# Differential attention on one core: GpSimd's part in the softmax pipeline, the place of a reciprocal, and where TensorE waits for two banks

## What is computed

```python
def diff_attn_rows(q1, q2, k1, k2, v, qpos, kpos, key_real, slopes, lam):
    dist = jnp.abs(qpos[:, None] - kpos[None, :]) * key_real[None, :]
    bias = -slopes[:, None, None] * dist[None]
    s1 = jnp.einsum('bqhd,bkhd->bhqk', q1, k1) * scale + bias
    s2 = jnp.einsum('bqhd,bkhd->bhqk', q2, k2) * scale + bias
    attn = jax.nn.softmax(s1, axis=-1) - lam * jax.nn.softmax(s2, axis=-1)
    return jnp.einsum('bhqk,bkhe->bqhe', attn, v)
```

## Time and profile before

| what | us |
|---|---|
| median of 3 runs | 1567.14 (1566.63 to 1567.72) |
| the profiled execution | 1568.71 |
| its span, first to last instruction | 1567.0 |
| TensorE busy over the span | 1527.6 (97%) |
| VectorE busy | 846.6 (54%) |
| ScalarE busy | 533.5 (34%) |
| GpSimd busy | 242.5 (15%) |
| mean granted TensorE clock | 0.995 |

### The profile page before, as it was taken

How to read it: one execution, slowest core, us unless ns; L and a number is a source line. 1 busy time by engine, 2 the same in 40 slices (tenths; PEclk the granted TensorE clock), 3 DMA queues, 4 the chain that set the end, 5 groups by cost and what they waited for, 6 DMA issues and landing times.

```text
span 1567.0 us, 21117 instructions
## 1 busy us (share of the span) xinstructions
PE 1527.6 (97%) x7380; PEld 1239.3 (79%) x7380; DVE 846.6 (54%) x1521; ACT 533.5 (34%) x942; POOL 242.5 (15%) x190
## 2 busy tenths in 40 slices
PE   7999999999999999999999999999999999999997
PEld 6867886877788888887699778788777888888876
DVE  5577895466554355345754283444665543553454
ACT  5124445533322222222511264444333221321223
POOL 2323334340000000000002373222400000000000
PEclk9999999999999999999999899999999999999999
DMA  6524420033333333322323201210333333333322
GB/s 149 149 54 122 148 58 1 8 89 107 93 94 98 90 94 94 102 87 83 91 81 93 55 15 55 68 54 28 102 99 91 97 94 94 94 94 94 94 81 94
DMA packets 250859, 132.61 MB, mean 85 GB/s; under 512 B 21289, under 2 KB 247717, under 8 KB 250798
## 3 DMA queue, kind: packets, MB, share of 16 engines
q1 hardware_dynamic: 248574, 123.92, 27.9%
q0 software_dynamic: 2144, 7.77, 1.6%
q10 hardware_dynamic: 80, 0.14, 0.0%
HBM read 129.67 MB, written 6.38 MB: 87 GB/s over the span
## 4 chain that ended last, share of the span: by engine, by line
PE 89%; DVE 5%; issue 2%; ACT 2%; DMA 1%; POOL 0%; SPq 0%; DVEq 0%; ACTq 0%
PE psL L1706 60%; PE psL L1845 11%; PE psS L1706 5%; PE psT L1854 2%; PE psL L1973 1%; PE psS L2117 1%; PE psS L1950 1%; PE psS L1880 1%; DMA xin<-in_x 1%; PE psS L1893 1%; PE psS L2057 1%; PE psL L2075 1%; DVE wl L1032 1%; PE psS L2094 1%; PE psS L2058 0%
## 5 line engine op out<-in xcount | busy, mean ns | idle before, releaser
L1706 PE MATMUL psL<-hn,wh 128*128 128x512 f32 x1680 | 529.0, 396 | 1.1 <-POOL wl L573 0.9
L1706 PEld LDWEIGHTS psL<-hn,wh 128*128 128x128 f32 x1680 | 314.1, 188 | 77.3 <-issue 1.4
L697 ACT ACTIVATE wh<-stage 128x1024 fp32r<-128x1024 f32 (+3 forms) x250 | 243.2, 973 | 325.6 <-PE psL L1706 232.8
L1706 PE MATMUL psL<-hn,wl 128*128 128x512 f32 x840 | 330.5, 393 | 0.0
L1032 DVE TENSOR_TENSOR wl<-stage,wh 128x1024 fp32r<-128x1024 f32 (+1 forms) x168 | 201.1, 1197 | 90.9 <-ACT wh L697 86.2
L1706 PE MATMUL psL<-hid,wh 128*128 128x512 f32 x704 | 222.1, 396 | 4.8 <-DVE wl L1032 4.8
L573 POOL TENSOR_TENSOR wl<-stage,wh 128x1024 fp32r<-128x1024 f32 (+2 forms) x82 | 156.8, 1913 | 326.5 <-ACT wh L697 326.5
L1706 PEld LDWEIGHTS psL<-hn,wl 128*128 128x128 f32 x840 | 158.0, 188 | 35.8
L1845 PE MATMUL psL<-hn,wh 128*128 128x512 f32 x496 | 172.8, 429 | 1.9 <-POOL wl L573 1.8
L1706 PEld LDWEIGHTS psL<-hid,wh 128*128 128x128 f32 x704 | 130.8, 187 | 40.7 <-DVE wl L1032 5.9
L1706 PE MATMUL psL<-hid,wl 128*128 128x512 f32 x352 | 138.8, 394 | 0.0
(11 more groups left out here) (381 smaller groups left out, 1982.4 us busy)
## 6 DMA issues: line engine op xcount, KB each, us to landing
stage<-in_w_in SPq DMA_DIRECT2D x54, 512.0 KB, 3.9
stage<-in_w_ffn_gate SPq DMA_DIRECT2D x22, 512.0 KB, 3.8
stage<-in_w_ffn_up SPq DMA_DIRECT2D x22, 512.0 KB, 3.8
stage<-in_w_ff_gate SPq DMA_DIRECT2D x22, 512.0 KB, 3.8
stage<-in_w_ff_up SPq DMA_DIRECT2D x22, 512.0 KB, 3.8
stage<-in_w_out SPq DMA_DIRECT2D x16, 512.0 KB, 3.9
stage<-in_w_ffn_down SPq DMA_DIRECT2D x16, 512.0 KB, 3.8
stage<-in_w_ff_down SPq DMA_DIRECT2D x16, 512.0 KB, 3.9
```

Of the source, the lines that this page charges most:

```text
L697: act.activation(wh[:, b, 0:n], stage[:, b, 0:n], ACT.Copy).then_inc(hi[b], 1)
L1706: ins = pe.matmul(dst, w[:, b, k * P:(k + 1) * P], x[:, part, k, c0:c1], start=k + n == 0, stop=k == kc - 1 and n == 2)
```

## The change

Five edits in the stage df, and the diff below is complete but for context.

- There is a second bias tile: `biasD0` and `biasD1`, used by even and odd blocks. The work on them is cut into units of one head (`bias_unit`), and the unit of block i, from block 2 on, waits only for the end of block i-2. The first three units lie between the `wl` tiles of `qb2`, three more ahead of the stage's steps, and the rest one to a step.
- The copy of the 16 meta columns moves from ScalarE to GpSimd (`stack_maps_meta`).
- GpSimd's eight `bias_window` instructions are spread: two to a step behind the copies of units 2 and 3, one to a step behind those of units 12 to 15. The `wl` tile of `gates2` comes behind all of them, so behind the last unit's copy.
- VectorE takes the reciprocal of unit j-1 between the two maps of unit j, with a semaphore `recip_ok` in place of the link.
- TensorE's wait for the two banks of `psL` moves from the head of the stage to step 3, ahead of the first instruction that writes them.

```diff
--- before.py
+++ after.py
@@ -293,6 +293,7 @@
         PT2, o = at("PT2", [P, 2, NB * P], o)
         m8d, o = at("m8d", [P, 2, P], o)
         vm8, o = at("vm8", [P, 5, NH, META], o)
+        biasD1, o = at("biasD1", [P, 4, NKEY], o)
         assert o <= hn0
 
 
@@ -350,7 +351,8 @@
         vbM, o = at("vbM", [P, NH * HD], o)
         qbT, o = at("qbT", [P, 4, SEQ], o)
         dist, o = at("dist", [P, DIST], o)
-        biasD, o = at("biasD", [P, 4, NKEY], o)
+        biasD0, o = at("biasD0", [P, 4, NKEY], o)
+        biasD = (biasD0, biasD1)
         o1 = o
         biasW, o = at("biasW", [P, NH, META + WIN2 + META], o1)
         vaT, o2 = at("vaT", [P, 4, NKEY], o1)
@@ -433,6 +435,7 @@
         h_sq, h_sq2, hg_hi, hg_lo = [sem(n) for n in "h_sq h_sq2 hg_hi hg_lo".split()]
         biasD_ok, biasW_ok, dist_ok, df_sum, y_sq, lam_e = [
             sem(n) for n in "biasD_ok biasW_ok dist_ok df_sum y_sq lam_e".split()]
+        recip_ok = sem("recip_ok")
         fin_gain, fin_rms, fin_out = sem("fin_gain"), sem("fin_rms"), sem("fin_out")
         fin_t, fin_ok = [sem("fin_t0"), sem("fin_t1")], [sem("fin_ok0"), sem("fin_ok1")]
 
@@ -643,13 +646,21 @@
             pool.iota(dist[:], pattern=[[-1, DIST]], base=3 * P, channel_multiplier=1,
                       allow_small_or_imprecise_dtypes=True).then_inc(dist_ok, 1)
 
-            def bias_block(i):
-
-                if i:
-                    pool.wait_ge(ph["df"]["neg"], 8 * i)
-                for h in range(4):
-                    pool.tensor_scalar(biasD[:, h, META:NKEY], dist[:, 3 * P - P * i:3 * P - P * i + SEQ],
-                                       -(2.0 ** (-8.0 * (h + 1) / 4)), None, ALU.mult).then_inc(biasD_ok, 1)
+            def bias_unit(j):
+
+                i, h = divmod(j, 4)
+                if i >= 2:
+                    pool.wait_ge(ph["df"]["neg"], 8 * (i - 1))
+                pool.tensor_scalar(biasD[i % 2][:, h, META:NKEY], dist[:, 3 * P - P * i:3 * P - P * i + SEQ],
+                                   -(2.0 ** (-8.0 * (h + 1) / 4)), None, ALU.mult).then_inc(biasD_ok, 1)
+
+            def stack_maps_meta(u):
+
+                i, h = divmod(u, 4)
+                pool.wait_ge(df_sum, u + 1)
+                if h == 0 and i >= 2:
+                    pool.wait_ge(ph["df"]["pt"], META_TURN[4][i - 2] + 1)
+                pool.tensor_copy(m8d[:, i % 2, h * META:(h + 1) * META], W6[:, u % 3, 0, 0:META]).then_inc(ph["df"]["meta"], 1)
 
             def bias_window(h0, h1):
                 for h in range(h0, h1):
@@ -664,19 +675,34 @@
             pool.tensor_copy(vm8[:, 4], vbT[:, 0:META].unsqueeze(1).broadcast_to([P, NH, META])).then_inc(vm8_ok, 1)
             low_pair("qa2", 1)
             pool.wait_ge(dist_ok, 2)
-            pool.memset(biasD[:, :, 0:META], 0.0)
-            low_pair("qb2", 0)
-            low_pair("qb2", 1)
-            bias_block(0)
-            bias_block(1)
+            for tile in biasD:
+                pool.memset(tile[:, :, 0:META], 0.0)
+            low("qb2", 0, 0)
+            bias_unit(0)
+            low("qb2", 0, 1)
+            bias_unit(1)
+            low("qb2", 1, 0)
+            bias_unit(2)
+            low("qb2", 1, 1)
+            for j in range(3, 6):
+                bias_unit(j)
+            pool.wait_ge(zeros, 2)
+            stack_maps_meta(0)
+            bias_unit(6)
+            stack_maps_meta(1)
+            bias_unit(7)
             pool.wait_ge(nat_t, 3)
             pool.wait_ge(dist_ok, 3)
             pool.memset(biasW[:, :, 0:META], 0.0)
             pool.memset(biasW[:, :, META + WIN2:], 0.0)
-            bias_window(0, NH // 2)
-            bias_block(2)
-            bias_window(NH // 2, NH)
-            bias_block(3)
+            for u in range(2, 16):
+                stack_maps_meta(u)
+                if 4 <= u < 12:
+                    bias_unit(u + 4)
+                elif u < 4:
+                    bias_window(2 * u - 4, 2 * u - 2)
+                else:
+                    bias_window(u - 8, u - 7)
             lows("gates2")
             lows("br2")
 
@@ -953,15 +979,6 @@
                 if j < 16:
                     for m in range(2):
                         softmax_unit(p, 2 * j + m, W6[:, j % 3, m, :], 2 * j + m)
-                if 2 <= j < 18:
-                    u = j - 2
-                    i, h = divmod(u, 4)
-                    act.wait_ge(df_sum, u + 1)
-                    if u == 0:
-                        act.wait_ge(zeros, 2)
-                    if h == 0 and i >= 2:
-                        act.wait_ge(p["pt"], META_TURN[4][i - 2] + 1)
-                    act.activation(m8d[:, i % 2, h * META:(h + 1) * META], W6[:, u % 3, 0, 0:META], ACT.Copy).then_inc(p["meta"], 1)
                 for n, u, i in turns_at(j - 2, 4):
                     take_turn(p, n, P if u is None else NB * P, PT2)
             units = list(window2_units())
@@ -1591,22 +1608,30 @@
                     take_scaled(name, i, 1, dst[:, 2 * i + 1, :], R, QSCALE)
 
             p = ph["df"]
+
+            def reciprocal_of(u):
+                v.wait_ge(ph["df"]["p"], 2 * u + 2)
+                v.reciprocal(st[:, 6, 0:1], rsum[:, 2 * u + 1:2 * u + 2]).then_inc(recip_ok, 1)
+
             for j in range(16 + 5):
                 if j < 16:
                     i, h = divmod(j, 4)
                     for m in range(2):
                         u = 2 * j + m
+                        if m and j:
+                            reciprocal_of(j - 1)
                         v.wait_ge(p["s"], u + 1)
                         v.wait_ge(biasD_ok, 4 * i + h + 1)
                         if j >= 3 and m == 0:
                             v.wait_ge(p["pt"], TURN[4][j - 3] + 1)
                             v.wait_ge(p["meta"], j - 2)
                         biased(p, u, as_halves(W6[:, j % 3, m, :], NKEY), two_banks(psS[:, 2 * m:2 * m + 2, :], NKEY),
-                               as_halves(biasD[:, h, :], NKEY), -TAKEN, u)
+                               as_halves(biasD[i % 2][:, h, :], NKEY), -TAKEN, u)
+                if j == 16:
+                    reciprocal_of(15)
                 if 1 <= j < 17:
                     u = j - 1
-                    v.wait_ge(p["p"], 2 * u + 2)
-                    dv.link(v.reciprocal(st[:, 6, 0:1], rsum[:, 2 * u + 1:2 * u + 2]))
+                    v.wait_ge(recip_ok, u + 1)
                     dv.link(v.scalar_tensor_tensor(out=st[:, 6, 1:2], in0=rsum[:, 2 * u:2 * u + 1], scalar=st[:, 6, 0:1], in1=neglam[:],
                                                    op0=ALU.mult, op1=ALU.mult))
                     v.scalar_tensor_tensor(out=W6[:, u % 3, 0, :], in0=W6[:, u % 3, 1, :], scalar=st[:, 6, 1:2], in1=W6[:, u % 3, 0, :],
@@ -2041,8 +2066,6 @@
             products("qa2", hn, first=1)
             products("qb2", hn)
 
-            for b in range(2):
-                pe.wait_ge(ev[b], PAIR0["gates2"])
             pe.wait_ge(nat_taken, 3)
             p = ph["df"]
             for j in range(16 + 4):
@@ -2063,6 +2086,9 @@
                     else:
                         pe.wait_ge(df_sum, u + 1)
                         turned(p, n, W6[:, u % 3, 0, :], [META + P * c for c in range(NB)])
+                if j == 3:
+                    for b in range(2):
+                        pe.wait_ge(ev[b], PAIR0["gates2"])
                 for n, u, i in turns_at(j - 3, 4):
                     pe.wait_ge(p["ptx"], n + 1)
                     if u is None:
```

## The result

The changed kernel takes 1561.49 us in the median of 6 executions (1558.65 to 1564.14), beside 1566.69 for the kernel before (6 executions, 1565.86 to 1567.72). The ratio is 0.9966, with a 95% interval from 0.9954 to 0.9978.

What follows compares the result with a forecast made beforehand. TensorE, busy 97% of the span, was taken to bound the kernel and df's steps; 0.6 + 1.36 + 0.25 + 0.3, and 0.1 for small collisions, made 2.6 us, so 1564.5 us, range 1561.8 to 1566.8.

Steps and rivals of the forecast that it cites:

- If the clock returns at the same time: Head of df: with the half-clock stretch ending at 902.0 as before, 1.0 us of lead saves only about 0.6 us.
- The granted clock at 0.50 for 10 us: Sign in df's profile after: 1.2 GHz for 10 us; any other length moves the time by half the difference.
- The bank wait: Head of df: scores start 1.0 us earlier with the wait at step 3; 0.6 us gained, between 0.3 and 1.0.
- The halving: Head of df: 1.0 us of lead at 1.2 GHz is work that takes 0.5 us at 2.4 GHz.
- The tile: Step 13 of df: the gates2 wl tile no longer holds VectorE's line 1610; 1.36 us gained.
- The biases: Steps of df: GpSimd's biases and VectorE's line 1610 miss each other, about 0; the second tile gives nothing by itself.
- The rival in which each bias holds the lock to its end: Steps of df: biases block line 1610, 1.2 us in eight steps; 1565.7 to 1566.9 us, chance 8%.
- The meta copy: Three meta turns in df: moving it off ScalarE gains 0.25 us; it takes 0.2 us on GpSimd.
- The reciprocal: VectorE's steps in df: 0.13 us without its link, shrinking a step by 0.07; 0.3 us gained, between -0.3 and 0.6.
- GpSimd at the end: End of df: the wl tile ends at 945.7 or 946.0, covered by 0.3 to 0.6 us before TensorE asks.
- GpSimd never became the bound: Rival, VectorE's meta wait before first maps: a copy over 1.1 us delays ten steps; 1571.5 us at 1.8, chance 4%.
- The first rival: Head of df: the slow stretch loses a third of its 10.1 us; 4.3 us gained, 1562.8 us, chance 25%.

Runs made afterwards that it cites:

- e5: The kernel before with one more GpSimd wait, so the first wl tile of the gates follows the last difference; 1564.65 us, ratio 0.9992.
- e1: The kernel before with only TensorE's bank wait moved to step 3; 1565.48 us, ratio 0.9994.
- a2: The changed kernel measured again, unchanged; 1561.14 us in the median of 5, ratio 0.9965.
- e3: The kernel before with only the reciprocal moved between the maps; 1567.41 us, ratio 1.0003.
- a4: The changed kernel with the meta copy back on ScalarE, GpSimd only waiting for the same differences; 1562.44 us, ratio 0.9963.
- after: The changed kernel with all five edits, in its first measurement; 1561.49 us, ratio 0.9966.
- e4: The changed kernel with the bank wait back at the head of the stage; 1563.89 us, ratio 0.9974.

## Why the prediction was wrong

**The step that failed** is "If the clock returns at the same time", with its sign "The granted clock at 0.50 for 10 us". I took the 10.1 us of one execution for a property of both kernels and made the whole sum inside it. Two things were lost by that: what the edits give at full clock, 3.6 us instead of 2.6, and that the changed kernel has less of 1.2 GHz on average (a mean clock of 0.9971 against 0.9956). The first of them can be added up: the five-piece table allows the sum at full clock, against the kernels with the old code in each piece (e5 for 0 to 12 and the tail, e1 for 12 to 15):

| term | predicted | at full clock |
|---|---|---|
| start of the stage (bank wait) | 0.6 | 0.87 |
| units 0 to 4 | nothing | 0.54 |
| units 4 to 12, biases, copy and reciprocal | 0.65 | 0.45 + 0.71 |
| units 12 to 15, the tile, with the rest | 1.36 | 1.52 |
| unit 15 to the last yn | nothing | -0.06 |
| behind the stage | nothing | -0.45 |
| sum | 2.6 | 3.6 |

- *The bank wait*: 1.95 us became 1.08. The halving can hold only in an execution with a slow stretch, and no pair of runs tests it there. The mechanism was right, and the term was mis-sized by 0.3.
- *Units 0 to 4*: missing from my sum. At full clock TensorE has only scores there, so VectorE's step is the bound, and it shrank. One step of a2 lasts 2.25 us from map to map. At half clock TensorE hides that, and since I looked at the stage only at half clock, I saw a TensorE bound that is not the rule. The table divides the 0.54 us: 0.08 are the reciprocal's (e3, 9.89 instead of 9.97), 0.07 the meta copy's (a4 against a2, 9.50 and 9.43), and the 0.39 left are those of GpSimd's new order beside the reciprocal (9.89 against 9.50).
- *The tile*: 1.36 predicted, 1.36 measured by e5. Right, mechanism and size.
- *The biases*: I said "so about 0" for their collisions and nothing for the second tile. Against a4, where the copy is as before, units 4 to 12 still gain 0.34 + 0.35 with the reciprocal, some 0.5 us without it. In units 4 to 12 of e5 two factor instructions took 0.31 and 0.60 us instead of 0.22 and two differences 1.0 instead of 0.77, each at the start of a bias; in a2 one factor took 0.43 and nothing else was held. So collisions that I had put at about 0 cost VectorE some 0.9 us there and cost 0.2 now. How much of the gain this is, and how much the biases' new place in time, the runs do not divide. The rival in which each bias holds the lock to its end is refuted: units 4 to 12 got shorter and in the trace of after the factor instruction is above 0.22 us in one of their steps alone (0.42).
- *The meta copy*: 0.25 predicted, 0.5 in the stage; its cost of 0.20 us on GpSimd was right. (0.1 at each of three turns would also have been 0.3.) I priced TensorE's wait by the time from one ScalarE instruction to the next, but the copy also waited there. The -0.45 behind the stage has no row of before that could have told it.
- *The reciprocal*: 0.3 predicted, 0.24 measured in the steps; 0.07 us in the middle, at the cheap end of the bound.
- *GpSimd at the end*: the tile was done some 0.6 us ahead of need, as estimated. GpSimd never became the bound.

At full clock that makes 3.6 us, and 5.2 and 5.7 were measured. The rest is 1.6 to 2.1 us, with an error of about 1 us or more for each measurement. The mean granted clock of the changed kernel is 0.9971 over its 11 executions, and over the 37 of the table above the rise is clear of the noise. What it is worth is an estimate. 0.0015 more of 1563 us is 4.7 us less at 1.2 GHz; in this stage a slow stretch of 6.8 to 10.2 us costs 2.6 to 3.0 us (12.01 against 9.43, 12.98 against 9.97), and at that price the 4.7 us are worth 1.4 to 1.8. Among executions of one kernel the time falls by only 0.34 us for each 0.001 of clock, which would make it 0.5. The rest beyond that may be luck, of the start-up for instance. The first rival, a shorter slow stretch with 1562.8 us at 25%, came nearest. Less time at 1.2 GHz is what the runs show, but its reason, that the missing gap shortens the stretch, is not supported by e1 and e4.

**The range** was too narrow for the same reason: the low end, 1561.8, allowed one shorter stretch with some terms at their better ends, though executions of one kernel scatter by up to 2.6 us (standard deviation) by themselves, which the three times of before (1.1 us apart) did not show.

## What to carry to other kernels

A stretch at a low clock in one profile is one draw; compare the mean clocks of many executions before a gain is put down to it or to luck. Work the sum out at both clocks and look for the engine that is the bound at each; the one that hides behind a slow TensorE comes to light at the full clock. Cut traces at marks and compare piece by piece when single executions scatter more than the change is worth: a piece repeats to 0.1 us where the totals scatter by 1 to 2. And place a long GpSimd instruction that reads SBUF where VectorE has no instruction with two SBUF inputs to do: a factor on one element in each partition stood for 1.6 to 2.0 us behind it. Useful work spread into the thin first steps of a pipeline can pay (2.5 us by the traces here), where filler brought nothing that could be measured.

## What the runs showed of the hardware

- The same program has a stretch at 1.2 GHz in the stage in one execution and none in another (after and a2). At the head of the stage it lasted 6.8 or 10.2 us, with no gap of TensorE over 0.83 us in the 8 us ahead of it; in e3 it came at 933 us, for 3.4 us, behind a gap of 1.50. I had expected the place and length to repeat.
- The lock between VectorE and GpSimd is not the same for all of GpSimd's instructions. A `tensor_tensor` of 2.35 us held the factor instruction to its end. A `tensor_scalar` of 128x512 (1.49 us) held it only in its first 0.40 us: the factor of the earlier trace rows that began 0.03 us behind the start of the bias ended 0.62 us behind it, and one that began 0.40 us behind, in e3, took its usual 0.22. A window bias of 128x384 (1.17 us) held it for 0.3 us: the factor, 0.55 us as the longest, ended 0.52 us behind its start. The rows, from e3 and after:

```profile
926.54 1.49 POOL L652 TENSOR_SCALAR biasD<-dist 128x512 f32<-128x512 f32 x1
926.94 0.22 DVE L1619 SCALAR_TENSOR_TENSOR st<-rsum,st,neglam 128x1 f32<-128x1 f32 x1
...
935.53 0.55 DVE L1635 SCALAR_TENSOR_TENSOR st<-rsum,st,neglam 128x1 f32<-128x1 f32 x1
935.56 1.17 POOL L667 TENSOR_SCALAR biasW<-tmp 128x384 f32<-128x384 f32 x1
```

- A reciprocal of one element in each partition costs 0.07 us in a running queue, and 0.20 with a wait for its own end.
- With 16 copies moved from ScalarE's program to GpSimd's, ScalarE starts 0.30, 0.08 and 0.08 us late in a loop some 580 us behind the stage that has the same code, in all eight traces of such kernels and in none of the six others. It costs the program 0.45 us.
